# Attention scores in 64x64 quarters, and a ninth gate/up block by seven products, in a one-core decoder layer

## Chip, core and metric

The kernel runs on one NeuronCore of a Trainium2 chip. The metric is the device time of one execution in microseconds. All products run on TensorE (PE); VectorE (DVE), ScalarE (ACT), GpSimd (POOL) and the DMA queue of SyncE (SP) feed it and read its banks.

## What is computed

One layer of a hybrid decoder, 512 tokens, 1024 features, float32:

```python
h = rms_norm(x, g_mix[l]);  z = h @ w_in[l]          # q, k, v, u, gate_a, gate_s
a = dilated_attention(q, k, v, g_q[l], g_k[l])       # windows (128,1), (512,4), (2048,16), 8 heads of 64
y = gelu(s5_ssm(u, ...))
s_out = (y @ w_glu_a[l]) * sigmoid(y @ w_glu_b[l])
mix = sigmoid(gate_a) * (a @ w_attn_proj[l]) + sigmoid(gate_s) * s_out
x = x + mix @ w_out[l]
h2 = rms_norm(x, g_ffn[l])
x = x + (silu(h2 @ w_ffn_gate[l]) * (h2 @ w_ffn_up[l])) @ w_ffn_down[l]     # 2816 hidden features
```

Scores are masked: with dilation 1, query q of a block sees keys q to 127 of the block before and keys 0 to q of its own.

## The kernel before, in words

The order of the work is written out by hand, one program for each engine, with semaphores between them. Each engine works strictly in its program's order. Weights come in tiles of 256 rows by 512 columns (`w_raw`, four buffers). ACT rounds a tile to `w_hi` (`hi`, L654), DVE subtracts to `w_lo` (`lo`, L660), two buffers each, and PE multiplies in three terms: hi by hi, hi by lo, lo by hi.

**Attention.** A loop goes over four pairs of heads. In it PE has ten steps `u`. Even steps up to 6 begin with `scores(i, n)` for query block n = u/2: the two heads lie in partitions 0 to 63 and 64 to 127 of `qT` and `kT` and write banks 4 and 5 of PSUM. A block needs three products for each head: dilation 1 (for n of 1 to 3 over 256 keys, the block before and its own), dilation 4 (128 keys) and dilation 16 (128 keys, where only classes of 32 positions see each other). Each step then has one or two products of the gate projection (six matmuls of 512 columns each), and `turn_prob(i, u - 1)`: three transposes of a unit's probabilities into bank 6. A unit is one head of one block, so 8 a pair. Steps 5 and 9 end with `values` of two blocks. DVE reads the scores of each unit with two masked reductions (L1257, L1259), after which `misc_dve` reaches `md_scores(unit)`; ACT takes the exponentials (L801, L804) and copies the transposed probabilities (L818). `scores` waits for its bank head by head:

```python
                    if n:
                        pe.wait_ge(misc_dve, MD_S + md_scores(2 * n - 2 + h) + MD_PAIR * i)
```

On DVE, step 4 ends with a `lo` of a gate tile, and the reductions of unit 5 stand behind it; the `hi` that this `lo` waits for stands on ACT behind the L818 copy of unit 3.

**Gate and up.** The 2816 hidden features make 11 blocks of 256. `FP = 3` of them are plain: `ffn(f, j)` has four tiles j of 24 matmuls of 512 columns (L1832) into banks 0 to 3, and DVE takes the banks with `columns_out` (L1390). The norm of `h2` is only known late: `x1_sums` stands on PE after tile 1, the spread of the norm over the partitions (L1847) after tile 2, and DVE copies it to `norm_all` (L1409). The other 8 blocks take seven products for eight (Strassen and Winograd), `seven(f)`: 14 steps of 12 matmuls of 256 columns (L1870). For each step i, DVE and ACT round an operand of weights (`op_hi`, `op_lo` L1427), of which some are sums that POOL makes (`block_sums`) once tiles 0 and 2 of the block have landed. Once, ahead of the first such block, DVE makes the other side: the normalised activations (`normed`, L1415, eight), four differences of them (`difference`, L1486), and the low parts of seven partners (`partner_lo`, L1423) with `partner_hi` on ACT (L894). SP issues the block's tiles (`blocks`, L451) as `lo` of the plain tiles frees their buffers: tile 2 of the first such block after `lo` of the third tile of the last plain block.

Of the kernel before, what the change touches and what calls it, by code (L numbers as in the profile page):

```python
# [14 lines left out]
P = 128  # L15
# [3 lines left out]
KT = DM // P  # L19
# [26 lines left out]
W_FFN = W_OUT + 8  # L46
FP = 3
W_DOWN = W_FFN + 4 * FP
# [14 lines left out]
def build(nc, t):  # L63

    with ExitStack() as ctx:
# [599 lines left out]
        def _(act):  # L665
# [221 lines left out]
            def partner_hi(i):  # L887
                if i in (0, 5, 6):
                    act.wait_ge(hn_done, KT)
                else:  # L890
                    act.wait_ge(t_done, {1: 2, 2: 3, 3: 4, 4: 1}[i])
                if i >= 3:
                    act.wait_ge(gemm_steps, 4 * (W_DOWN - 4 + i - 3) + 4)
                nc.scalar.activation(partner(i, 0), partner_raw(i), ACT.Copy).then_inc(b_hi_done, 1)  # L894
# [40 lines left out]
            silus(0, 2)  # L935
            for j in range(1, 5):
                hi(W_FFN + j + 4, j)
                if j >= 3:
                    partner_hi(j - 3)
            for m in range(2):  # L940
                act.wait_ge(ffn_evac, 4 + m + 1)
                nc.scalar.activation(sg[:, m], sg[:, m], ACT.Silu).then_inc(silu_done, 1)
            for j in range(1, 4):
                hi(W_FFN + j + 8, j)
                if j < 3:
                    partner_hi(j + 1)
            for i in range(3):
# [8 lines left out]
            for m in range(2):  # L956
                act.wait_ge(ffn_evac, 8 + m + 1)
                nc.scalar.activation(sg[:, m], sg[:, m], ACT.Silu).then_inc(silu_done, 1)
# [22 lines left out]
        def _(dve):  # L981
# [427 lines left out]
            V.tensor_copy(norm_all[:, :], ps[:, 5]).then_inc(norm2_eps, 1)  # L1409
            lo(W_FFN + 4, 4)  # L1410
            dve.wait_ge(norm2_eps, 2)
            swiglu(0)

# [66 lines left out]
            def difference(n):  # L1480
# [5 lines left out]
                V.tensor_tensor(t_raw[n], a, b, ALU.subtract).then_inc(t_done, 1)  # L1486

            lo(W_FFN + 5, 1)
            for k in range(KT):
                normed(k)  # L1490
            lo(W_FFN + 6, 2)
            for n in range(3):
                difference(n)
            lo(W_FFN + 7, 3)
            difference(3)
            partner_lo(0)
            lo(W_FFN + 8, 4)
            partner_lo(1)
            swiglu(1)
            for j in range(1, 4):  # L1500
                lo(W_FFN + j + 8, j)
                if j < 3:
                    partner_lo(j + 1)
            for i in range(3):
# [35 lines left out]
        def _(pe):  # L1540
# [172 lines left out]
            def scores(i, n):  # L1713

                heads = (slice(0, 64), slice(64, 128))
                k0 = 0 if n else P
                q = slice(n * P, (n + 1) * P)
                for h in range(2):
                    if n:
                        pe.wait_ge(misc_dve, MD_S + md_scores(2 * n - 2 + h) + MD_PAIR * i)  # L1720
                    T.matmul(ps[:, 4 + h, k0:256], qT[heads[h], 0, q], kT[heads[h], 0, n * P - P + k0:n * P + P],  # L1721
                             start=True, stop=True)
                for g in (1, 2):
                    for h in range(2):
                        ins = T.matmul(ps[:, 4 + h, (g + 1) * P:(g + 2) * P], qT[heads[h], g, q], kT[heads[h], g, q],  # L1725
                                       start=True, stop=True)
                        if g == 2:
                            ins.then_inc(scores_done, 1)

            def turn_prob(i, u):  # L1730
                pe.wait_ge(prob_done, 8 * i + u + 1)
                if u:
                    pe.wait_ge(misc_act, MA_Y + ma_probT(u - 1) + MA_PAIR * i)
                for x in range(0 if u // 2 else 1, 3):
                    ins = T.transpose(ps[:, 6, x * P:(x + 1) * P], prob[u % 4][:, x * P:(x + 1) * P], ident[:, :])  # L1735
                ins.then_inc(prob_turned, 1)
# [78 lines left out]
            for c in range(2):  # L1815
                run(columns(W_OUT + 4 * c, 4, by_feature, h_acts, by_dve(DE_GLU + 4) if c == 0 else lambda m: None,
                            split_rows(mix_lo_done, 0), 4 * c))
            def ffn(f, j):
                w = W_FFN + j + 4 * f
                pe.wait_ge(w_lo_done, w + 1)  # L1820
                for m in range(4):
                    if j == 0:
                        if isinstance(f, int):
                            pe.wait_ge(dve_evac, DE_MIX + m + 1)
                        else:
                            pe.wait_ge(ffn_evac, 4 * f - 3 + m)
                    if isinstance(f, int) and m == 0:
                        pe.wait_ge(h2_lo_done, 2 * j + 2)
# [14 lines left out]
            ins.then_inc(x1_sums, 1)  # L1843
            ffn(0, 2)
            pe.wait_ge(norm2_done, 1)
            for n in range(TB):
                ins = T.matmul(ps[:, 5, n * P:(n + 1) * P], norm_row[:, n:n + 1].to_broadcast([P, P]), ident[:, :],  # L1847
                               start=True, stop=True)
            ins.then_inc(norm2_spread, 1)
            ffn(0, 3)  # L1850
            with pe.Fori(1, FP) as f:
                for j in range(4):
                    ffn(f, j)
# [91 lines left out]
```

## Time and profile before

| what | value |
|---|---|
| median of 3 runs | 857.26 us (856.96 to 857.64) |
| the profiled execution | 857.08 us |
| its span, first to last instruction | 855.3 us |
| PE busy | 848.7 us (99%) |
| DVE, ACT, POOL busy | 571.8, 361.2, 250.2 us |
| mean DMA rate | 127 GB/s |

The profiled execution lies 0.18 us under the median, and 1.8 us of it lie outside the span. Busy shares are means over the whole span; which engine waits for which is read from single stretches.

### The profile page before, as it was taken

To read this page: it belongs to the slowest core of one execution; us is meant where nothing else is said; L and a number is where in the kernel's file an instruction comes from. 1 tells how busy PE (TensorE), PEld (TensorE's weight loads), DVE (VectorE), ACT (ScalarE), POOL (GpSimd) and SP (SyncE) were. 2 spreads that over 40 slices of the span, in tenths; PEclk is the share of its full clock that TensorE was granted. 3 is DMA by queue.
4 is the path that set the end of the run, shared out by engine and by line. 5 is a ranking of instruction groups with operands and counts; after the bars stand their busy time and mean duration, and the time that the engine had idled before them with its cause. 6 is when DMAs were issued, how large, how long until landed. Compare 5 with 4: busy or idle time off the path is not lost.

```text
span 855.3 us, 15076 instructions
## 1 busy us (share of the span) xinstructions
PE 848.7 (99%) x5171; PEld 729.5 (85%) x5171; DVE 571.8 (67%) x790; ACT 361.2 (42%) x575; POOL 250.2 (29%) x266
## 2 busy tenths in 40 slices
PE   9999999999999999999999999999999999999998
PEld 8888788888887888888877888889999999888886
DVE  6458976567934564545587666889999999533334
ACT  6312353313345665756333343444545544222221
POOL 0689995010020000001220220056666664000000
PEclk9999999999999999999999999999999999999999
DMA  8439237634465543512635232332334333322212
GB/s 312 148 107 238 75 123 147 216 121 137 132 220 161 172 139 107 169 50 78 179 118 197 78 105 89 100 88 85 113 109 115 105 98 114 103 93 92 92 70 98
DMA packets 103494, 108.87 MB, mean 127 GB/s; under 512 B 11712, under 2 KB 69296, under 8 KB 103328
## 3 DMA queue, kind: packets, MB, share of 16 engines
q1 hardware_dynamic: 96544, 94.25, 35.4%
q10 hardware_dynamic: 5504, 10.52, 3.8%
q0 software_dynamic: 1408, 3.61, 1.9%
q8 instruction: 22, 0.36, 0.2%
q14 instruction: 16, 0.13, 0.0%
HBM read 94.38 MB, written 13.96 MB: 127 GB/s over the span
## 4 chain that ended last, share of the span: by engine, by line
PE 93%; DVE 4%; issue 1%; POOL 1%; ACT 0%; DMA 0%; SPq 0%; ACTq 0%; POOLq 0%
PE ps L1555 46%; PE ps L1870 18%; PE ps L1890 13%; PE ps L1832 6%; PE ps L1750 2%; PE ps L1779 1%; PE ps L1721 1%; PE ps L1735 1%; DVE early L1075 1%; PE ps L1725 1%; PE ps L1591 1%; PE ps L1602 1%; DVE late L1537 1%; DVE w_lo L1427 1%; DVE h_lo L1423 1%
## 5 line engine op out<-in xcount | busy, mean ns | idle before, releaser
L660 DVE TENSOR_TENSOR w_lo<-w_raw,w_hi 128x1024 fp32r<-128x1024 f32 x109 | 139.3, 1278 | 204.7 <-ACT w_hi L654 204.7
L654 ACT ACTIVATE w_hi<-w_raw 128x1024 fp32r<-128x1024 f32 x109 | 115.3, 1058 | 282.1 <-PE ps L1555 160.3
L1555 PE MATMUL ps<-w_hi,hT_hi 128*128 128x512 f32 x280 | 109.6, 392 | 0.7 <-DVE early L993 0.7
L1555 PE MATMUL ps<-w_hi,hT_lo 128*128 128x512 f32 x280 | 109.0, 389 | 0.0
L1555 PE MATMUL ps<-w_lo,hT_hi 128*128 128x512 f32 x280 | 109.0, 389 | 0.0
L1555 PE MATMUL ps<-hT_hi,w_hi 128*128 128x512 f32 x224 | 91.8, 410 | 0.0
L1555 PE MATMUL ps<-hT_hi,w_lo 128*128 128x512 f32 x224 | 87.7, 392 | 0.0
L1555 PE MATMUL ps<-hT_lo,w_hi 128*128 128x512 f32 x224 | 87.4, 390 | 0.0
L498 POOL TENSOR_TENSOR early<-early 128x16 f32<-128x16 f32 (+5 forms) x125 | 76.0, 608 | 9.7
L1870 PE MATMUL ps<-h_hi,w_hi 128*128 128x256 f32 x256 | 72.8, 285 | 0.6 <-DVE w_lo L1427 0.5
L1870 PE MATMUL ps<-h_lo,w_hi 128*128 128x256 f32 x256 | 72.4, 283 | 0.0
L1870 PE MATMUL ps<-h_hi,w_lo 128*128 128x256 f32 x256 | 72.4, 283 | 0.0
L1870 PE MATMUL ps<-hT_hi,wx_t 128*128 128x256 f32 x384 | 71.7, 283 | 0.0
L1890 PE MATMUL ps<-hT_hi,w_hi 128*128 128x512 f32 x176 | 68.5, 389 | 0.0
L1890 PE MATMUL ps<-hT_lo,w_hi 128*128 128x512 f32 x176 | 68.5, 389 | 0.0
L1890 PE MATMUL ps<-hT_hi,w_lo 128*128 128x512 f32 x176 | 68.5, 389 | 0.0
L1555 PEld LDWEIGHTS ps<-w_hi,hT_hi 128*128 128x128 f32 x280 | 52.6, 188 | 12.8 <-DVE early L993 1.5
L1555 PEld LDWEIGHTS ps<-w_lo,hT_hi 128*128 128x128 f32 x280 | 52.6, 188 | 11.1
L1555 PEld LDWEIGHTS ps<-w_hi,hT_lo 128*128 128x128 f32 x280 | 52.6, 188 | 10.8
L1870 PEld LDWEIGHTS ps<-hT_hi,wx_t 128*128 128x128 f32 x384 | 61.0, 192 | 0.0
L1870 PE MATMUL ps<-hT_lo,wx_t 128*128 128x256 f32 x192 | 54.3, 283 | 0.0
L1870 PEld LDWEIGHTS ps<-h_hi,w_hi 128*128 128x128 f32 x256 | 49.1, 192 | 1.3 <-DVE w_lo L1427 0.9
(249 smaller groups left out, 1793.0 us busy)
## 6 DMA issues: line engine op xcount, KB each, us to landing
w_raw<-in_w_in SPq DMA_DIRECT2D x108, 256.0 KB, 3.7
w_raw<-in_w_ffn_down SPq DMA_DIRECT2D x44, 256.0 KB, 2.8
w_raw<-in_w_ffn_gate SPq DMA_DIRECT2D x64, 128.0 KB, 2.2
w_raw<-in_w_ffn_up SPq DMA_DIRECT2D x64, 128.0 KB, 2.4
z_d<-early ACTq DMA_DIRECT2D x7, 1024.0 KB, 5.0
late<-z_d SPq DMA_DIRECT2D x96, 64.0 KB
w_raw<-in_w_out SPq DMA_DIRECT2D x16, 256.0 KB, 3.0
late<-z_d SPq DMA_DIRECT2D x12, 256.0 KB
```

Of the source, the lines that this page charges most:

```text
L498: tab(pool.tensor_tensor(out, a, b, op))
L654: nc.scalar.activation(w_hi[:, j % WSPL], w_raw[:, j % WRAW], ACT.Copy).then_inc(w_hi_done, 1)
L660: nc.vector.tensor_tensor(w_lo[:, j % WSPL], w_raw[:, j % WRAW], w_hi[:, j % WSPL].bitcast(F32), ALU.subtract).then_inc(w_lo_done, 1)
L1075: V.tensor_tensor(out, a, b, op).then_inc(table_prods, 1)
L1423: V.tensor_tensor(partner(i, 1), partner_raw(i), partner(i, 0).bitcast(F32), ALU.subtract).then_inc(b_lo_done, 1)
L1427: V.tensor_tensor(op_at(i, 1), op_raw(i, p), op_at(i, 0).bitcast(F32), ALU.subtract).then_inc(op_lo_done, 1)
L1537: V.tensor_tensor(y_out[:, m], x1[:, m], ps[:, m], ALU.add).then_inc(out_done, 1)
L1555: ins = T.matmul(ps[:, bank0 + m], lhsT, rhs, start=first and h == 0 and k == 0, stop=last and h == 1 and k == 2)
L1750: ins = T.matmul(ps[h * HD:(h + 1) * HD, 7, n % 2 * 256 + s * P:n % 2 * 256 + (s + 1) * P], vt[b][:, g, key, h * HD:(h + 1) * HD], turned_ ...
L1832: ins = T.matmul(ps[:, m], (w_hi, w_lo)[b][:, j % WSPL, at_w:at_w + P], (h2_hi, h2_lo)[a][:, 2 * j + h, :], start=j == 0 and h == 0 and k ...
L1870: ins = T.matmul(ps[:, BANK[i], g * 256:g * 256 + 256], op_at(i, b)[:, h * 256 + g * P:h * 256 + g * P + P], partner(i, a)[:, 2 * p + h], ...
L1890: ins = T.matmul(ps[:, m], (w_hi, w_lo)[b][:, j % WSPL, m * P:(m + 1) * P], h_acts[a][:, j % 2, :], start=first and k == 0, stop=last and ...
```

## The change

Three edits are made together.

- `scores` for blocks 1 to 3 is cut in two halves of 64 queries, c = 0 and 1. With the two heads this gives products of 64 rows by 64 columns of the array, four for each dilation. Each half takes only the keys that its queries can see: 192 of 256 for dilation 1, 128 for dilation 4, 64 of 128 for dilation 16.
- The waits of `scores` for its banks are gone. In their place `turn_prob` waits ahead of its third transpose, for units 0, 2 and 4, until DVE has read unit 1, 3 or 5.
- `FP` is 2. The spread of the second norm moves inside the third tile of the first plain block, and the preparation of the partners is reordered on ACT and DVE to fit beside one plain block.

```diff
-FP = 3
+FP = 2
...
             silus(0, 2)
-            for j in range(1, 5):
+            for j in range(1, 4):
                 hi(W_FFN + j + 4, j)
-                if j >= 3:
-                    partner_hi(j - 3)
-            for m in range(2):
-                act.wait_ge(ffn_evac, 4 + m + 1)
-                nc.scalar.activation(sg[:, m], sg[:, m], ACT.Silu).then_inc(silu_done, 1)
-            for j in range(1, 4):
-                hi(W_FFN + j + 8, j)
                 if j < 3:
-                    partner_hi(j + 1)
+                    partner_hi(j - 1)
+            for i in (2, 3):
+                partner_hi(i)
             for i in range(3):
                 op_hi(FP, 0, i, True)
...
             V.tensor_copy(norm_all[:, :], ps[:, 5]).then_inc(norm2_eps, 1)
-            lo(W_FFN + 4, 4)
             dve.wait_ge(norm2_eps, 2)
-            swiglu(0)
...
+            for k in range(4):
+                normed(k)
+            lo(W_FFN + 4, 4)
+            for k in range(4, KT):
+                normed(k)
+            columns_out(0)
             lo(W_FFN + 5, 1)
-            for k in range(KT):
-                normed(k)
-            lo(W_FFN + 6, 2)
+            gated(0)
             for n in range(3):
                 difference(n)
+            partner_lo(0)
+            lo(W_FFN + 6, 2)
+            difference(3)
+            partner_lo(1)
             lo(W_FFN + 7, 3)
-            difference(3)
-            partner_lo(0)
-            lo(W_FFN + 8, 4)
-            partner_lo(1)
-            swiglu(1)
-            for j in range(1, 4):
-                lo(W_FFN + j + 8, j)
-                if j < 3:
-                    partner_lo(j + 1)
+            for i in (2, 3):
+                partner_lo(i)
             for i in range(3):
                 op_lo(FP, 0, i)
...
-                k0 = 0 if n else P
-                q = slice(n * P, (n + 1) * P)
-                for h in range(2):
-                    if n:
-                        pe.wait_ge(misc_dve, MD_S + md_scores(2 * n - 2 + h) + MD_PAIR * i)
-                    T.matmul(ps[:, 4 + h, k0:256], qT[heads[h], 0, q], kT[heads[h], 0, n * P - P + k0:n * P + P],
-                             start=True, stop=True)
-                for g in (1, 2):
-                    for h in range(2):
-                        ins = T.matmul(ps[:, 4 + h, (g + 1) * P:(g + 2) * P], qT[heads[h], g, q], kT[heads[h], g, q],
-                                       start=True, stop=True)
-                        if g == 2:
-                            ins.then_inc(scores_done, 1)
+                for g in range(3):
+                    for c in range(2 if n else 1):
+                        first, count = ((64 * c, 192) if n else (P, P), (256, P), (384 + 64 * c, 64) if n else (384, P))[g]
+                        key = n * P + first - (P, 256, 384)[g]
+                        m = slice(64 * c, 64 * c + 64) if n else slice(0, P)
+                        for h in range(2):
+                            ins = T.matmul(ps[m, 4 + h, first:first + count], qT[heads[h], g, n * P + m.start:n * P + m.stop],
+                                           kT[heads[h], g, key:key + count], start=True, stop=True)
+                            if g == 2 and c == (1 if n else 0):
+                                ins.then_inc(scores_done, 1)
...
                 for x in range(0 if u // 2 else 1, 3):
+                    if x == 2 and u in (0, 2, 4):
+                        pe.wait_ge(misc_dve, MD_S + md_scores(u + 1) + MD_PAIR * i)
                     ins = T.transpose(ps[:, 6, x * P:(x + 1) * P], prob[u % 4][:, x * P:(x + 1) * P], ident[:, :])
...
-            ffn(0, 2)
+            ffn(0, 2, (0, 1))
             pe.wait_ge(norm2_done, 1)
             for n in range(TB):
                 ins = T.matmul(ps[:, 5, n * P:(n + 1) * P], norm_row[:, n:n + 1].to_broadcast([P, P]), ident[:, :],
                                start=True, stop=True)
             ins.then_inc(norm2_spread, 1)
+            ffn(0, 2, (2, 3))
             ffn(0, 3)
```

PE before, from `turn_prob` of unit 4 (step 5) to the scores of block 3 (step 6); `late` is the arena that holds `prob`, `qT`, `kT` and the values:

```order
L1735 MATMUL ps<-ident,late 128x128 [waits misc_act]
L1735 MATMUL ps<-ident,late 128x128 x2
L1743 ISA [waits class_turned,misc_act]
L1750 MATMUL ps<-late 64x128 [waits zt_v_in]
L1750 MATMUL ps<-late 64x128 x5
L1750 MATMUL ps<-late 64x128 [waits class_turned,misc_act]
L1750 MATMUL ps<-late 64x128 x7
L1720 REGISTER_ALU
L1721 MATMUL ps<-late 128x256 [waits misc_dve]
L1720 REGISTER_ALU
L1721 MATMUL ps<-late 128x256 [waits misc_dve]
L1725 MATMUL ps<-late 128x128 x4
```

PE of the change at the same place, where the lines are numbered by the changed file:

```order
L1730 MATMUL ps<-ident,late 128x128 [waits misc_act]
L1730 MATMUL ps<-ident,late 128x128
L1729 REGISTER_ALU
L1730 MATMUL ps<-ident,late 128x128 [waits misc_dve]
L1738 ISA [waits class_turned,misc_act]
L1745 MATMUL ps<-late 64x128 [waits zt_v_in]
L1745 MATMUL ps<-late 64x128 x5
L1745 MATMUL ps<-late 64x128 [waits class_turned,misc_act]
L1745 MATMUL ps<-late 64x128 x7
L1718 MATMUL ps<-late 64x192 x4
L1718 MATMUL ps<-late 64x128 x4
L1718 MATMUL ps<-late 64x64 x4
```

The wait for `misc_dve` has moved from the scores of block 3 to the third transpose, ahead of the 14 value products. In both programs it asks for unit 5.

DVE before, from the copy of `norm_all` on; `late` holds `x1`, `hn`, the differences and the blocks' results:

```order
L1409 COPY norm_all<-ps 128x512 [waits norm2_spread]
L660 TENSOR_TENSOR w_lo<-w_raw,w_hi 128x1024 [waits w_hi_done]
L1390 TENSOR_TENSOR late<-ps,norm_all 128x512 [waits gemm_steps,norm2_eps]
L1390 TENSOR_TENSOR late<-ps,norm_all 128x512 [waits gemm_steps] x3
L1397 TENSOR_TENSOR late<-late 128x512 [waits ffn_evac,silu_done] x2
L660 TENSOR_TENSOR w_lo<-w_raw,w_hi 128x1024 [waits w_hi_done]
L1415 SCALAR_TENSOR_TENSOR late<-late,small,norm_all 128x512 x8
L660 TENSOR_TENSOR w_lo<-w_raw,w_hi 128x1024 [waits w_hi_done]
```

DVE of the change from the same copy to the `lo` of tile 2 of the last plain block:

```order
L1404 COPY norm_all<-ps 128x512 [waits norm2_spread]
L1408 SCALAR_TENSOR_TENSOR late<-late,small,norm_all 128x512 [waits norm2_eps]
L1408 SCALAR_TENSOR_TENSOR late<-late,small,norm_all 128x512 x3
L660 TENSOR_TENSOR w_lo<-w_raw,w_hi 128x1024 [waits w_hi_done]
L1408 SCALAR_TENSOR_TENSOR late<-late,small,norm_all 128x512 x4
L1385 TENSOR_TENSOR late<-ps,norm_all 128x512 [waits gemm_steps] x4
L660 TENSOR_TENSOR w_lo<-w_raw,w_hi 128x1024 [waits w_hi_done]
L1392 TENSOR_TENSOR late<-late 128x512 [waits ffn_evac,silu_done] x2
L1479 TENSOR_TENSOR late<-late 128x1024 [waits hn_done]
L1479 TENSOR_TENSOR late<-late 128x1024 [waits t_done,hn_done] x2
L1416 TENSOR_TENSOR hT_lo<-late,hT_hi 128x1024 [waits b_hi_done]
L660 TENSOR_TENSOR w_lo<-w_raw,w_hi 128x1024 [waits w_hi_done]
```

The eight `normed` now stand ahead of `columns_out` (L1385), and all the preparation lies beside one plain block, where two had it before.

## Rows read from the trace of the kernel before

**Rows 1.** The page: the span; PE's busy tenths and granted clock in 40 slices.
```profile
span 855.3 us, 15076 instructions
PE   9999999999999999999999999999999999999998
...
PEclk9999999999999999999999999999999999999999
```

**Rows 2.** Timeline of PE, scores of block 1: start, us, rows*columns.
```profile
261.54 0.70 PE L1721 MATMUL ps<-late 64*128 64x256 f32 x4
262.07 0.61 PE L1725 MATMUL ps<-late 64*128 64x128 f32 x8
262.61 0.50 PE L1555 MATMUL ps<-hT_hi,w_hi 128*128 128x512 f32 x1
```

**Rows 3.** Timeline of PE, products of the SSM that already run as quarters.
```profile
237.66 1.16 PE L1699 MATMUL ps<-early 64*64 64x64 f32 x64
238.75 0.38 PE L1706 MATMUL ps<-early 128*128 128x128 f32 x1
```

**Rows 4.** Timeline of PE, steps 4 to 6 of the first pair.
```profile
270.17 0.49 PE L1735 MATMUL ps<-ident,late 128*128 128x128 f32 x3
...
271.88 0.49 PE L1735 MATMUL ps<-ident,late 128*128 128x128 f32 x3
272.31 1.75 PE L1750 MATMUL ps<-late 128*64 128x128 f32 x28
273.98 0.84 PE L1721 MATMUL ps<-late 64*128 64x256 f32 x4
```

**Rows 5.** Timelines of ACT and DVE at the same place.
```profile
270.69 0.49 ACT L818 ACTIVATE late<-ps 128x384 f32<-128x384 f32 x1
271.08 1.05 ACT L654 ACTIVATE w_hi<-w_raw 128x1024 fp32r<-128x1024 f32 x1
...
272.16 1.23 DVE L660 TENSOR_TENSOR w_lo<-w_raw,w_hi 128x1024 fp32r<-128x1024 f32 x1 [2.12 <-ACT w_hi L654]
...
273.64 0.42 DVE L1259 CUSTOM_DVE_ANT_0 late<-ps,masks 128x256 f32<-128x256 f32 x1
```

**Rows 6.** Timelines of DVE and PE: the end of unit 3, the transposes of unit 2.
```profile
265.52 0.09 DVE L1259 DVE_READ_ACCUMULATOR2_ANT late<- 128x1 f32 x1
...
267.16 0.49 PE L1735 MATMUL ps<-ident,late 128*128 128x128 f32 x3
```

**Rows 7.** Timeline of PE in the gate/up stage, at the starts that count.
```profile
519.49 1.05 PE L1847 MATMUL ps<-ident,norm_row 128*128 128x128 f32 x8
...
525.85 0.39 PE L1832 MATMUL ps<-h_hi,w_hi 128*128 128x512 f32 x1
...
569.37 0.28 PE L1870 MATMUL ps<-hT_hi,wx_t 128*128 128x256 f32 x1
...
578.68 0.39 PE L1870 MATMUL ps<-h_hi,w_hi 128*128 128x256 f32 x1 [0.52 <-DVE w_lo L1427]
...
611.19 0.28 PE L1870 MATMUL ps<-hT_hi,wx_t 128*128 128x256 f32 x1
...
711.99 0.28 PE L1870 MATMUL ps<-hT_hi,wx_t 128*128 128x256 f32 x1
```

**Rows 8.** Timeline of DVE in the same stage.
```profile
520.58 0.69 DVE L1409 COPY norm_all<-ps 128x512 f32<-128x512 f32 x1 [4.91 <-PE ps L1847]
...
529.00 5.38 DVE L1415 SCALAR_TENSOR_TENSOR late<-late,small,norm_all 128x512 f32<-128x512 f32 x8
...
535.44 3.88 DVE L1486 TENSOR_TENSOR late<-late 128x1024 f32<-128x1024 f32 x3
...
554.40 1.23 DVE L660 TENSOR_TENSOR w_lo<-w_raw,w_hi 128x1024 fp32r<-128x1024 f32 x1 [2.43 <-ACT w_hi L654]
...
568.18 2.47 DVE L1390 TENSOR_TENSOR late<-ps,norm_all 128x512 f32<-128x512 f32 x4
...
576.85 1.78 DVE L1427 TENSOR_TENSOR w_lo<-late,w_hi 128x512 fp32r<-128x512 f32 x1
```

More of the change, by code:

```diff
@@ L956, in _ @@
             for m in range(2):
-                act.wait_ge(ffn_evac, 8 + m + 1)
+                act.wait_ge(ffn_evac, 4 * FP - 4 + m + 1)
                 nc.scalar.activation(sg[:, m], sg[:, m], ACT.Silu).then_inc(silu_done, 1)
@@ L1817, in _, with ffn @@
                             split_rows(mix_lo_done, 0), 4 * c))
-            def ffn(f, j):
+            def ffn(f, j, columns=range(4)):
                 w = W_FFN + j + 4 * f
                 pe.wait_ge(w_lo_done, w + 1)
-                for m in range(4):
+                for m in columns:
                     if j == 0:
-                        if isinstance(f, int):
+                        if f == 0:
                             pe.wait_ge(dve_evac, DE_MIX + m + 1)
@@ L1826, in ffn @@
                             pe.wait_ge(ffn_evac, 4 * f - 3 + m)
-                    if isinstance(f, int) and m == 0:
+                    if f == 0 and m == 0:
                         pe.wait_ge(h2_lo_done, 2 * j + 2)
@@ L1849, in _ @@
             ins.then_inc(norm2_spread, 1)
+            ffn(0, 2, (2, 3))
             ffn(0, 3)
-            with pe.Fori(1, FP) as f:
+            for f in range(1, FP):
                 for j in range(4):
```

## The prediction

> **What bounds the kernel now.** I read the page first. PE is busy in every slice of the span [rows 1], so a change pays by what it takes from PE's program, and any wait that it puts into that program is lost unless PE would have waited there anyway. Then I read PE's timeline in the two stages that are edited, for the price of each product, and beside it the timelines of ACT and DVE, for when the semaphores that PE waits for are reached.
>
> **Scores by quarters: what is removed.** Scores of a block from 1 to 3 now take from 261.54 to 262.61, 1.07 us [rows 2]. Each float32 product shows as two matmuls, and those of the two heads start together: the eight matmuls of 128 columns are four pairs, (0.61 - 0.27) / 3 = 0.11 apart (a matmul of 128 columns lasts 0.27 of that), which is 0.83 ns a column and 5 ns more. So the stream is 2 x (256 + 128 + 128) columns, and what is left of 1.07 is a first weight load of about 0.11 and the drain ahead of the next matmul.
>
> Do four quarters also start together? The SSM's products answer: 64 matmuls of 64x64 in 1.16 us, of which the last lasts 0.22 [rows 3]. The starts fill 0.94 us, that is 0.058 for each four: 64 columns at 0.83 ns and 5 ns more. Four quarters cost what one does. A block's scores then are a weight load of half the columns (0.053), 2 x 0.165 for 192 columns, 2 x 0.112 for 128, one step of 0.058 to the last four, 0.02 for their skew, and 0.15 to the next matmul (237.66 + 0.94 to 238.75 [rows 3]): 0.83 us. Saved: 0.24 us, twelve times (three blocks, four pairs), **-2.9 us**. The bounds are -3.2 (the columns and the half weight load in full: 0.213 + 0.054 each) and +4.9 (halves one behind the other, below).
>
> **The moved wait.** This is the term that decides. In the pair shown, the transposes of unit 4 start at 271.88, and the third at 271.88 + 0.49 - 0.27 = 272.10 [rows 4]. It will wait for DVE to have read unit 5, whose second reduction ends at 273.64 + 0.42 = 274.06 [rows 5]. Nothing in the change brings that forward: the reductions stand behind a `lo` (272.16), that behind a `hi` on ACT (271.08), that behind the copy of unit 3 (270.69), and that behind PE's transposes of unit 3, which begin at 270.17 and end near 270.66 [rows 4, 5]. From there to the third transpose PE has one product, which the change leaves as it is. The cheaper scores pull both sides forward alike. So PE stands from 272.10 to about 274.13 (0.07 for the semaphore), and a transpose that starts anew pays its weight load, some 0.1: **2.13 us**. What is queued behind it on PE are all the value products (28 matmuls, 1.68 us) and the scores of block 3; DVE and ACT wait for these scores, but are 2 us ahead by then and cost nothing more.
>
> Before, the same semaphore was asked for after the value products, at 273.98, and cost little: the four dilation 1 matmuls there take 0.84 instead of 0.70 [rows 2, 4], 0.14 us. That goes away. The waits moved for units 0 and 2 are free: for unit 2, unit 3 is read at 265.61 and its transposes start at 267.16 [rows 6]; unit 0 has the same order of work. So a pair gains 3 x 0.24 + 0.14 = 0.86 and loses 2.13: +1.27, and in four pairs, which have one instruction stream and the same spacing, **+5.0 us**. Bounds of the wait: 0 (met in time) to 2.4 us (if the rest of a matmul's latency is exposed).
>
> **One more block by seven products.** A plain block takes (569.37 - 525.85) / 2 = 21.76 us, 0.2267 for each of 96 matmuls and 5.44 a tile; a block by seven products takes (711.99 - 611.19) / 5 = 20.16 us [rows 7]. In steady state the swap gives **-1.60 us**. The spread moves on PE from behind tile 2 into its middle and costs PE the same.
>
> What has to be ready is the question. Put on the clock of before: the spread starts 12 matmuls sooner, at 519.49 - 2.72 = 516.77, and the copy of `norm_all` 1.09 later [rows 7, 8], at 517.86. DVE then runs, with durations from [rows 5, 8]: copy and its own semaphore to 518.65; four `normed` at 0.66 to 521.3; the `lo` of tile 4, whose `hi` cannot start before tile 2 ends (525.85 - 5.44 = 520.41, and 0.2 + 1.05 for the `hi`), 521.7 to 522.85; four `normed` to 525.5; `columns_out` at 0.60 each (2.47 for four) to 527.9. The first of these frees bank 0 at 526.2, and PE wants it at 525.85 [rows 7]: **+0.4 us**. The `hi` of tile 5 stands on ACT behind two silus (an estimate of 0.6 each, from 0.49 for the 384 columns of L818), so its `lo` runs 528.5 to 529.65; `gated` 1.2, as two of `columns_out`; three differences 3.8; the first `partner_lo` 1.15; and the `lo` of tile 6, on which SP waits to fetch tile 2 of the first block by seven products, ends at 537.0. PE wants tile 6 at 526.25 + 10.88 = 537.13, just after.
>
> From that `lo` on everything is in the order of before: fetch, POOL's sums, operands, the last partner. Before, it ended at 554.40 + 1.23 = 555.63, 13.74 ahead of the first L1870 at 569.37, and the operand of step 6 was ready at 576.85 + 1.78 = 578.63, 23.0 later, when PE had just begun to wait (578.68) [rows 7, 8]. Now the plain blocks end at 526.25 + 21.76 = 548.0, so the `lo` is 11.0 ahead, not 13.74, and step 6 starts 2.74 later against its block than before: **+2.7 us**. Of this some 0.3 and 0.6 fall ahead of steps 3 and 5, whose operands come out of the same chain. Before, these 11 us had two plain blocks to hide in. Bounds: 0 (the fetch and the sums were not what bound) to 5. Sum of this part: -1.6 + 0.4 + 2.7 = **+1.5 us**.
>
> **Sum.** +5.0 + 1.5 (1.55 before rounding) = +6.6 us. On the profiled execution's own 857.08 (855.3 of span and 1.8 around it) that is 863.7; on the median of 857.26, 863.8, which I give.
>
> **A rule that speaks against quarters.** In rows, 64 small matmuls start in 0.94 us, 15 ns each [rows 3], so the 24 matmuls of a block's scores are not bound by their number. The Trainium skill, page "TensorE: Matmul & The Clock Gate", section "Wait - 56ns, not 53.3ns?", says that where the engine's sequencer decodes matmuls itself it spends about 62 ns on each, which binds once the products are shorter than that. By that page 24 of them would take 1.5 us and the sum would come out near 874 us; the trace of this case does not agree with it.
>
> **Rivals.**
> - *The wait is met in time* (chance 0.07). Should unit 5 be read before the third transpose, the wait costs nothing; the point of decision is 272.10 against 274.06. Then attention gains 4 x 0.86 = 3.5, and with +1.5 the time is 855.3 us, faster. For it: DVE idles 2.12 us ahead of the `lo` [rows 5], so it has room. Against: that idleness is a wait for ACT, which the change does not touch.
> - *The preparation fits* (0.18). If fetch and sums follow the `lo` with slack, the third block's -1.6 stays whole: 857.26 + 5.0 - 1.6 = 860.7 us. For it: DVE does 11 us of work here and idled often. Against: PE already waited at step 6 with two blocks to prepare in [rows 7].
> - *The halves don't overlap* (0.05). Then 768 columns in place of 512 stream: the 0.82 us of stream become 1.23, +0.41 a block instead of -0.24, twelve times +7.8: 871.6 us. Against it: [rows 3].
> - *The preparation is later still* (0.10): a `lo` that misses its `hi`, or slower DVE work beside POOL, some 2.7 us more: 866.5 us.
>
> **How the numbers follow.** My forecast, stall and late preparation both, has 0.60, with a range of its own of 862 to 866. The range of 859.9 to 866.7 takes in the second and fourth rival and leaves out the first and third, 0.12, and tails of the forecast. A difference under 0.2% (1.7 us, 855.5 to 859.0) could not be told from no change here. Slower by more: 0.90 (forecast, rivals two to four, less 0.03 for cases in between); same 0.04 (half of the rival with the met wait lies about there); faster 0.06.
>
> **What the profile would show.** Right: PE idle ahead of the third transpose in step 5, about 2 us in each pair, released by DVE's L1259 or its successor; scores of blocks 1 to 3 at 0.83 us; the loop over pairs longer by 1.3 us each; the first block by seven products waiting some 3.5 us in sum, most at step 6. Wrong: no idle time there, quarters that start 0.16 apart in twos, or a first block without waits. The forecast would also fail if a stall of 2 us let PE's granted clock, full in all slices of before [rows 1], fall to its lower level afterwards.

## The result, and the profile after

The changed kernel takes **867.31 us** (median of 4 runs, 867.16 to 867.51), against 857.33 (4 runs) of the kernel before on the same chip: ratio 1.0115, interval 1.0101 to 1.0129. It is 10.0 us slower, where 6.6 were forecast, and 0.6 us past the end of the range. The profiled execution took 867.16 us, 10.1 more than that of before.

The page of the kernel after, to be laid beside [rows 1]: PE's busy tenths and its granted clock in 40 slices.

```profile
span 865.4 us, 15616 instructions
...
PE   9999999999999999999999999989999999999998
...
PEclk9999999999999999999999999999999999999999
```

PE is busy nearly everywhere, as before; the 27th slice, in gate/up, has lost a tenth. What else was lost is too thin for slices of 21.6 us, and stands in the timelines.

Timelines of PE and DVE of the kernel after, the first pair of heads, as [rows 2, 4, 5]: start, us.

```profile
261.88 0.89 PE L1718 MATMUL ps<-late 64*64 64x192 f32 x24
262.69 0.50 PE L1549 MATMUL ps<-hT_hi,w_hi 128*128 128x512 f32 x1
...
264.19 0.38 PE L1730 MATMUL ps<-ident,late 128*128 128x128 f32 x2
264.62 0.50 PE L1549 MATMUL ps<-hT_hi,w_hi 128*128 128x512 f32 x1
...
271.98 0.38 PE L1730 MATMUL ps<-ident,late 128*128 128x128 f32 x2
274.23 0.33 PE L1730 MATMUL ps<-ident,late 128*128 128x128 f32 x1 [1.87 <-DVE late L1254]
274.48 1.75 PE L1745 MATMUL ps<-late 128*64 128x128 f32 x28
276.16 0.89 PE L1718 MATMUL ps<-late 64*64 64x192 f32 x24
...
263.34 1.23 DVE L660 TENSOR_TENSOR w_lo<-w_raw,w_hi 128x1024 fp32r<-128x1024 f32 x1 [3.21 <-ACT w_hi L654]
...
272.26 1.23 DVE L660 TENSOR_TENSOR w_lo<-w_raw,w_hi 128x1024 fp32r<-128x1024 f32 x1 [2.08 <-ACT w_hi L654]
...
273.74 0.42 DVE L1254 CUSTOM_DVE_ANT_0 late<-ps,masks 128x256 f32<-128x256 f32 x1
```

The reader sees three things. The scores of a block take 0.82 us (261.88 to 262.69, rounded), where [rows 2] have 1.07. The third transpose starts at 274.23. Transposes follow each other 0.11 apart, so behind those of 271.98 and 272.09 it would have started at 272.20: it is 2.03 us late. DVE's L1254 begins its last reduction for unit 5 at 273.74, behind a `lo` at 272.26 that has waited for ACT. And from the transposes at 264.19 to the product at 264.62 it is 0.43 us: the product waits for the `lo` that began at 263.34. The same place in the kernel before:

```profile
264.11 0.38 PE L1735 MATMUL ps<-ident,late 128*128 128x128 f32 x2
264.29 0.50 PE L1555 MATMUL ps<-hT_hi,w_hi 128*128 128x512 f32 x1
```

There it was 0.18, so 0.25 are new here; over the four pairs it is 0.27 each.

The waits of the kernel after, PE's for the reductions: us in all, times, longest.

```profile
PE ps L1730 <- DVE late L1254: 7.5, 4, 1.9
```

Four waits, one in each pair, of 1.9 us. They are counted from the end of the transpose before, at 272.36 in the first pair; the next could have started at 272.20, as transposes overlap, so it is late by more than its wait. From one start of `scores(0)` to the next, a pair lasts 37.41, 37.37 and 38.98 us; before it was 35.95 to 35.97. The third stands out by 1.6 us. Windows of 4 us over that pair show why.

```profile
core 0: us, PE busy (x) PEld busy (x) DVE busy (x) ACT busy (x) POOL busy (x), PEclk, DMA share, GB/s
...
345.00:349.00 4.00, 2.13 (x13) 1.59 (x11) 1.91 (x5) 2.02 (x7) 0.00 (x0) 1.00 0.62 181
349.00:353.00 4.00, 4.00 (x42) 3.43 (x46) 0.00 (x0) 2.37 (x6) 0.00 (x0) 0.57 0.07 23
```

PE stood in the first window (busy 2.13 of 4 us), and in the next its granted clock is 0.57 on the mean: it was at the lower level, 1.2 GHz, from 349.04 to 352.45. The 28 value products of that pair fill 3.2 us instead of 1.7.

Timelines of PE, POOL and DVE of the kernel after in the gate/up stage, as [rows 7, 8].

```profile
534.18 0.47 PE L1827 MATMUL ps<-h_hi,w_hi 128*128 128x512 f32 x1 [0.37 <-DVE late L1385]
...
556.07 0.28 PE L1866 MATMUL ps<-hT_hi,wx_t 128*128 128x256 f32 x1
...
564.71 0.39 PE L1866 MATMUL ps<-h_hi,w_hi 128*128 128x256 f32 x1 [0.30 <-DVE w_lo L1420]
...
568.60 0.39 PE L1866 MATMUL ps<-h_hi,w_hi 128*128 128x256 f32 x1 [2.20 <-DVE w_lo L1420]
...
549.00 3.21 POOL L628 TENSOR_TENSOR late<-w_raw 128x512 f32<-128x512 f32 x1 [25.77 <-DMA w_raw<-in_w_ffn_up]
...
543.56 1.22 DVE L660 TENSOR_TENSOR w_lo<-w_raw,w_hi 128x1024 fp32r<-128x1024 f32 x1
...
550.37 0.69 DVE L1420 TENSOR_TENSOR wx_t<-w_raw,wx_t 128x512 fp32r<-128x512 f32 x1
554.28 1.10 DVE L1420 TENSOR_TENSOR wx_t<-late,wx_t 128x512 fp32r<-128x512 f32 x1 [3.22 <-ACT wx_t L906]
...
566.80 1.74 DVE L1420 TENSOR_TENSOR w_lo<-late,w_hi 128x512 fp32r<-128x512 f32 x1
```

At 534.18 PE has waited 0.4 us for `columns_out`. The first block by seven products starts at 556.07; its step 6 would be due 8.64 later (six steps of 1.44) at 564.71, but that is when step 5 begins, and step 6 follows at 568.60. Step 5 itself takes 1.44, so 2.45 us are step 6's own wait, for the operand that DVE has ready at 566.80 + 1.74 = 568.54. The `lo` at 543.56 is that of tile 6. POOL's first sum takes 3.21 us, and DVE, which was busy without a gap until 551.06, then waits 3.22 for what hangs on it. The same sum in the kernel before, begun while DVE was idle:

```profile
559.64 1.30 POOL L628 TENSOR_TENSOR late<-w_raw 128x512 f32<-128x512 f32 x1 [44.20 <-DMA w_raw<-in_w_ffn_up]
```

### The profile page after: what moved, and what is told of

Read it like the earlier page. It is cut to its first block, busy times and chain, and to the rows that moved or that the text cites. A ratio compares the mean times of both kernels' runs of the same rounds, so it can differ in the third digit from the quotient of the medians.

```text
span 865.4 us, 15616 instructions
## 1 busy us (share of the span) xinstructions
PE 846.7 (98%) x5387; PEld 729.6 (84%) x5387; DVE 581.2 (67%) x802; ACT 366.7 (42%) x585; POOL 265.5 (31%) x274
## 4 chain that ended last, share of the span: by engine, by line
PE 48%; DVE 4%; issue 1%; POOL 1%; ACT 1%; DMA 0%; SPq 0%; DVEq 0%; ACTq 0%; POOLq 0%
PE ps L1866 20%; PE ps L1886 13%; PE ps L1549 12%; PE ps L1827 2%; DVE late L1531 1%; DVE w_lo L1420 1%; DVE h_lo L1416 1%; DVE w_lo L660 0%; DVE late L1479 0%; PE ps L1745 0%; POOL late L628 0%; ACT w_hi L654 0%; DVE late L1385 0%; DVE late L1346 0%; DVE late L1408 0%
## 5 line engine op out<-in xcount | busy, mean ns | idle before, releaser
L660 DVE TENSOR_TENSOR w_lo<-w_raw,w_hi 128x1024 fp32r<-128x1024 f32 x105 | 132.6, 1263 | 198.8 <-ACT w_hi L654 198.6
L654 ACT ACTIVATE w_hi<-w_raw 128x1024 fp32r<-128x1024 f32 x105 | 111.1, 1058 | 267.8 <-PE ps L1549 165.2
L1866 PE MATMUL ps<-h_hi,w_hi 128*128 128x256 f32 x288 | 82.1, 285 | 3.3 <-DVE w_lo L1420 3.2
L1866 PE MATMUL ps<-h_hi,w_lo 128*128 128x256 f32 x288 | 81.5, 283 | 0.0
L1866 PE MATMUL ps<-h_lo,w_hi 128*128 128x256 f32 x288 | 81.5, 283 | 0.0
L1866 PE MATMUL ps<-hT_hi,wx_t 128*128 128x256 f32 x432 | 80.7, 283 | 0.0
L498 POOL TENSOR_TENSOR early<-early 128x16 f32<-128x16 f32 (+5 forms) x125 | 74.1, 593 | 9.7
L1866 PEld LDWEIGHTS ps<-hT_hi,wx_t 128*128 128x128 f32 x432 | 68.7, 192 | 0.0
L1866 PE MATMUL ps<-hT_lo,wx_t 128*128 128x256 f32 x216 | 61.1, 283 | 0.0
L1866 PEld LDWEIGHTS ps<-h_hi,w_hi 128*128 128x128 f32 x288 | 55.2, 192 | 4.4 <-DVE w_lo L1420 4.0
```

What stands on the lines that cost most here:

```text
L498: tab(pool.tensor_tensor(out, a, b, op))
L654: nc.scalar.activation(w_hi[:, j % WSPL], w_raw[:, j % WRAW], ACT.Copy).then_inc(w_hi_done, 1)
L660: nc.vector.tensor_tensor(w_lo[:, j % WSPL], w_raw[:, j % WRAW], w_hi[:, j % WSPL].bitcast(F32), ALU.subtract).then_inc(w_lo_done, 1)
L1866: ins = T.matmul(ps[:, BANK[i], g * 256:g * 256 + 256], op_at(i, b)[:, h * 256 + g * P:h * 256 + g * P + P], partner(i, a)[:, 2 * p + h], ...
```

## Experiments

Ratios are to the kernel before, run on the same chip in turn. Spacings, starts and falls of the clock are from the profiled execution of each. Where an edit isn't taken from the change's own diff, it is shown.

**1. Attention alone:** the kernel before with the new `scores` and the moved waits, both as in the change's diff; `FP = 3` and the gate/up stage stay as before.

> The attention part of the change alone: scores by quarters and the moved waits, three plain gate/up blocks as before. Theory A (the moved wait of unit 5 costs 2.09 us a pair, the quarters save 0.53 of a possible 0.79, the wait at the scores of block 3 gives back 0.15): 4 x 1.43 = +5.7, so 863.0 us, and up to 1.7 us more for each time that PE's granted clock falls to 1.2 GHz behind a stall. Theory B (the gate/up part is what costs, attention gains by its quarters): below 857.

Measured: 864.62 us, ratio 1.0081 (1.0066 to 1.0095), +7.4 us. Timeline of PE of this kernel, step 5 of the first pair:

```profile
271.60 0.38 PE L1736 MATMUL ps<-ident,late 128*128 128x128 f32 x2
273.84 0.33 PE L1736 MATMUL ps<-ident,late 128*128 128x128 f32 x1 [1.86 <-DVE late L1259]
274.10 3.01 PE L1751 MATMUL ps<-late 128*64 128x128 f32 x28
277.04 1.25 PE L1724 MATMUL ps<-late 64*64 64x192 f32 x24
```

and the window that holds it, in which the granted clock is 0.67 on the mean:

```profile
273.00:277.00 4.00, 3.16 (x29) 2.75 (x29) 0.78 (x5) 2.44 (x6) 0.00 (x0) 0.67 0.30 91
```

The same stall (the third transpose 2.03 us late), here with the lower clock behind it in the first pair (38.97 us, the others 37.36). So the fall isn't tied to the third pair: it comes behind one of four equal stalls.

**2. The moved waits alone, scores uncut,** on the kernel before.

```diff
                 for h in range(2):
-                    if n:
-                        pe.wait_ge(misc_dve, MD_S + md_scores(2 * n - 2 + h) + MD_PAIR * i)
...
                 for x in range(0 if u // 2 else 1, 3):
+                    if x == 2 and u in (0, 2, 4):
+                        pe.wait_ge(misc_dve, MD_S + md_scores(u + 1) + MD_PAIR * i)
```

> Scores as before, in whole products; only the waits are moved into the transposes. Theory A: a stall of about 2.1 us in each pair, 4 x (2.09 - 0.15) = +7.8, so 865.1 us and up to 1.7 more for each fall of the clock. Theory B (quarters cost by their number of instructions or by the wait for the gate tile, the wait is hidden): within 0.5 us of before.

Measured: 867.09 us, ratio 1.0106 (1.0090 to 1.0122), +9.9 us. Pairs last 39.56, 37.92 and 37.87 us: +1.93 without a fall of the clock, 1.6 more with one. Against experiment 1, quarters save only 0.5 a pair, not three times 0.26 = 0.78: the 0.27 of the wait for the `lo` go off it.

**3. Attention alone, with the wait for unit 5 moved behind most of the value products:** ahead of the last one of block 1. The diff is against experiment 1.

```diff
-                    if x == 2 and u in (0, 2, 4):
+                    if x == 2 and u in (0, 2):
                         pe.wait_ge(misc_dve, MD_S + md_scores(u + 1) + MD_PAIR * i)
...
                     for h in range(2):
+                        if n == 1 and blk == 3 and h == 1:
+                            pe.wait_ge(misc_dve, MD_S + md_scores(5) + MD_PAIR * i)
```

> Scores by quarters as in the change, but the wait for unit 5 stands ahead of the last value product of block 1, where PE comes about 1.8 us later. Theory A: the stall shrinks to some 0.3 us a pair, the quarters' 0.53 remain: 4 x -0.3 = -1.2, about 856.1 us. Theory B (quarters cost by themselves): 858 or more.

Measured: 856.93 us, ratio 0.9996 (0.9987 to 1.0005), granted clock 1.00 throughout the profiled execution. Timeline of PE:

```profile
271.65 0.49 PE L1736 MATMUL ps<-ident,late 128*128 128x128 f32 x3
272.07 2.26 PE L1753 MATMUL ps<-late 128*64 128x128 f32 x28
274.26 0.89 PE L1724 MATMUL ps<-late 64*64 64x192 f32 x24
```

The stall is gone, but 28 value products take 2.2 us instead of 1.7: the last still waits for unit 5. A pair lasts 35.82 us, 0.15 less than before. That shows the stall's place to be what decides, and that DVE's chain to unit 5 is the pair's bound once PE has caught up with it: cheaper scores alone only turn into a longer wait.

**4. Gate/up alone:** the changed kernel (`FP = 2` and the new order of the preparation) with `scores` and its waits put back as before.

> The gate/up part alone: two plain blocks, nine by seven products, spread inside the third tile; attention as before. Theory A (the first block by seven products waits for its preparation): -1.6 + 0.65 + 3.2 = +2.3, so 859.6 us, granted clock full throughout. Theory B (the part is good for its 1.6 us, and what it lost in the change was an after-effect of attention): 855.7.

Measured: 860.17 us, ratio 1.0032 (1.0020 to 1.0044), +2.9 us. With the +7.4 of experiment 1 that makes 10.3, and the whole change cost 10.0: the parts add, to within what one fall of the clock more or less makes. That the clock would be full throughout was wrong: in its windows of 555 to 560, 560 to 565 and 565 to 570 us the granted clock is 1.00, 0.66 and 1.00, behind the stall at step 6 (PE idle from 558.82 to 561.02).

**5. Attention alone, with DVE's `lo` of step 4 put behind the reductions of unit 5.** The waits stay where the change has them. The diff is against experiment 1.

```diff
-                        if u in (1, 4, 8):
-                            lo(W_GATE + (u + 1) // 3 + 2 - u // 8 + 4 * i, (u + 1) // 3 + 2 - u // 8)
+                        if u in (1, 5, 8):
+                            x = {1: 2, 5: 3, 8: 4}[u]
+                            lo(W_GATE + x + 4 * i, x)
```

> Attention part alone, all waits where the change has them, but on DVE the lo of the gate tile in step 4 stands behind the reductions of unit 5 and not ahead of them. Theory A (the stall is the wait for reductions that stand behind this lo): unit 5 is read near 270.3, the third transpose at 272.1 finds its semaphore reached, no idle time there and no fall of the clock. Quarters then save 0.27 + 0.26 + 0.15 a pair, those of block 1 nothing, since PE waits for the lo of a gate tile right behind them: 4 x -0.68 = -2.7, about 854.5 us. Theory B (the stall comes from something else on the way, such as PE's own wait for the exponentials): 862 or more stays.

Measured: 854.38 us, ratio 0.9970 (0.9959 to 0.9982). Timelines of PE and DVE:

```profile
271.78 0.49 PE L1737 MATMUL ps<-ident,late 128*128 128x128 f32 x3
272.20 1.75 PE L1752 MATMUL ps<-late 128*64 128x128 f32 x28
273.88 0.89 PE L1725 MATMUL ps<-late 64*64 64x192 f32 x24
...
270.56 0.09 DVE L1259 DVE_READ_ACCUMULATOR2_ANT late<- 128x1 f32 x1
272.05 1.23 DVE L660 TENSOR_TENSOR w_lo<-w_raw,w_hi 128x1024 fp32r<-128x1024 f32 x1 [1.41 <-ACT w_hi L654]
```

Unit 5 is read at 270.65, 1.3 us ahead of the third transpose; all three run together, values take 1.7 us, and the clock stays full. A pair lasts 35.30 us. One moved line on DVE turns +7.4 us into -2.5.

**6. The same, and on ACT the `hi` of step 1 put ahead of the copy of unit 0.**

```diff
+                        if u == 1:
+                            hi(W_GATE + 2 + 4 * i, 2)
                         if u >= 1:
...
-                        if u in (1, 4, 7):
+                        if u in (4, 7):
                             hi(W_GATE + u // 3 + 2 + 4 * i, u // 3 + 2)
```

> As the run before, and on ACT the hi of the gate tile in step 1 stands ahead of the copy of unit 0's transposed probabilities, so that its lo is ready some 0.9 us sooner. Theory A (the first quarters' saving of 0.26 a pair is eaten by PE's wait for that lo): another 4 x -0.26 = -1.0, about 853.5 us. Theory B (the 0.28 us on PE behind the transposes of unit 1 are a cost of quarters or of switching the array): same as the run before.

Measured: **853.05 us**, ratio 0.9957 (0.9943 to 0.9971), the fastest kernel here. Timelines of ACT and PE at the place where the changed kernel lost 0.28 us:

```profile
261.30 1.05 ACT L654 ACTIVATE w_hi<-w_raw 128x1024 fp32r<-128x1024 f32 x1
262.25 0.36 ACT L820 ACTIVATE late<-ps 128x256 f32<-128x256 f32 x1
...
264.10 0.38 PE L1739 MATMUL ps<-ident,late 128*128 128x128 f32 x2
264.23 0.48 PE L1558 MATMUL ps<-hT_hi,w_hi 128*128 128x512 f32 x1
```

The product starts 0.13 us after the first of its transposes, not 0.43. That shows the second missed term: the `hi` used to stand behind a copy that waits for PE's transposes, ahead of the scores, so that cheaper scores brought PE sooner to a `lo` that came no sooner.

**7. Gate/up alone, with the `lo` of tile 6 two operations sooner.**

```diff
-            for n in range(3):
+            for n in range(2):
                 difference(n)
-            partner_lo(0)
             lo(W_FFN + 6, 2)
+            difference(2)
+            partner_lo(0)
             difference(3)
```

> Gate/up part alone; the lo of tile 6, which lets SP fetch tile 2 of the first block by seven products, stands ahead of the third difference and the first partner and so ends some 2.4 us sooner. Theory A1 (as predicted: the chain from this lo over fetch and sums sets step 6): the wait at step 6 shrinks by as much, about 857.7 us. Theory A2 (POOL's first sum gets nowhere while DVE is busy without a gap, whenever its tiles land): the first sum ends where it did, and the time stays within 0.5 us of the gate/up part alone, 860.2.

Measured: 860.15 us, ratio 1.0037 (1.0023 to 1.0052), as experiment 4. Timelines of POOL and DVE:

```profile
540.30 4.59 POOL L628 TENSOR_TENSOR late<-w_raw 128x512 f32<-128x512 f32 x1 [24.20 <-DMA w_raw<-in_w_ffn_up]
...
543.07 0.69 DVE L1420 TENSOR_TENSOR wx_t<-w_raw,wx_t 128x512 fp32r<-128x512 f32 x1
```

The fetch lands sooner and the sum starts sooner (in experiment 4: 541.38, for 3.24 us), but it ends at 544.9 against 544.6: 1.14 us after DVE's run without a gap ended (543.75), as there (543.47). (The two executions are 0.5 us apart at the first block by seven products, so against it the sum starts some 1.6 us sooner.) This breaks the chain of my forecast, in which everything follows from the `lo` of tile 6.

**8. Gate/up alone, with POOL's first four sums made over 16 columns.** The kernel leaves out the rest of these sums (their buffers are zeroed beforehand), so it doesn't compute the whole block; it only shows what they cost.

```diff
-                pool.tensor_tensor(s1_f[p], a21, a22, ALU.add).then_inc(sum_done, 1)
+                few = (lambda a: a[:, 0:16]) if first and p == 0 else (lambda a: a)
+                pool.tensor_tensor(few(s1_f[p]), few(a21), few(a22), ALU.add).then_inc(sum_done, 1)
...
```

> Gate/up part alone; POOL makes the first four block sums over 16 columns in place of 512, the rest stays zero, so the output of that block is left out in part. Theory A (fetch and sums set the late operands of the first block): op 1 and 2 come some 3 us sooner, steps 3, 5 and 6 hardly wait, about -1.6 + 0.65 + 0.3 against before: 856.6 us. Theory B (DVE's own work for one plain block is what is too much): still 859 or more.

Measured: 856.34 us, ratio 0.9994 (0.9984 to 1.0003). Timelines of POOL and DVE:

```profile
540.66 2.26 POOL L629 TENSOR_TENSOR late<-w_raw 128x16 f32<-128x16 f32 x1 [23.80 <-DMA w_raw<-in_w_ffn_up]
543.00 0.22 POOL L631 TENSOR_TENSOR late<-late,w_raw 128x16 f32<-128x16 f32 x1
...
542.16 0.69 DVE L1424 TENSOR_TENSOR wx_t<-w_raw,wx_t 128x512 fp32r<-128x512 f32 x1
```

Even a sum of 16 columns, whose like takes 0.22 us, lasts 2.26 us and ends 0.07 after DVE's run (542.85). With the sums out of the way the stalls ahead of steps 3 and 5 are gone, and step 6 waits 0.58 us instead of 2.45: the sums are what binds the late preparation.

**9. The whole change, with both mends of attention** (the diffs of experiments 5 and 6).

> The whole change with attention mended as in the two attention runs (lo of step 4 behind unit 5, hi of step 1 ahead of the copy). If the parts add up: 853.05 us and the gate/up part's 2.9 make 856.0. If the gate/up part's late operands interact with the earlier start: off that by more than 0.8.

Measured: 856.14 us, ratio 0.9991 (0.9981 to 1.0000): experiments 6 and 4 summed (-3.8 and +2.9). The clock falls once, from 557.49 to 560.90, that is 0.25 us before the stall at step 6 ends (557.74). Of its eleven runs five have a mean granted clock of 1.000, so no fall, and four have 0.998, one fall; the five take 856.1 us on the mean, the four 857.1.

**10. Gate/up alone, POOL's sums of the second half held back to the seventh operand.**

```diff
-            pool.wait_ge(op_lo_done, 5)
+            pool.wait_ge(op_lo_done, 7)
             block_sums(FP, 1, True)
```

> Gate/up part alone, but POOL begins the second half's block sums only when all seven low parts of the first half are made, not after five. Theory (DVE and POOL take each other's time, so the sums of the second half stretch DVE's last operands of the first: 1.78, 2.30 and 1.75 us where 0.68, 1.21 and 0.68 are possible): the operand of step 6 comes 2.9 us sooner, but the sums of the second half come as much later and bring a wait of 1 to 2 us at its step 1 or 2: 858.2 us against 860.2. Rival (no contention, the chain is only in order): no change at step 6, 860.2 or more.

Measured: 859.98 us, ratio 1.0037 (1.0023 to 1.0051): expected 858.2, so a miss. Timeline of DVE, first of experiment 4, where POOL sums beside it:

```profile
555.29 1.78 DVE L1420 TENSOR_TENSOR w_lo<-w_raw,w_hi 128x512 fp32r<-128x512 f32 x1
557.00 2.30 DVE L1416 TENSOR_TENSOR h_lo<-late,h_hi 128x1024 fp32r<-128x1024 f32 x1
559.22 1.74 DVE L1420 TENSOR_TENSOR w_lo<-late,w_hi 128x512 fp32r<-128x512 f32 x1
```

and of this kernel, with PE's later wait:

```profile
555.04 0.69 DVE L1420 TENSOR_TENSOR w_lo<-w_raw,w_hi 128x512 fp32r<-128x512 f32 x1
555.65 1.22 DVE L1416 TENSOR_TENSOR h_lo<-late,h_hi 128x1024 fp32r<-128x1024 f32 x1
556.78 0.69 DVE L1420 TENSOR_TENSOR w_lo<-late,w_hi 128x512 fp32r<-128x512 f32 x1
...
562.42 0.38 PE L1865 MATMUL ps<-hT_hi,wx_t 128*128 128x256 f32 x1 [1.53 <-DVE wx_t L1420]
```

The three operations take 2.6 us instead of 5.8, and PE reaches step 6 without a wait at either 5 or 6. But the second half's operands are later by as much: its second step starts at 562.42, 1.7 late, and the next four are 1.7 apart instead of 1.44. The contention is real, and its cost only changes its place. The equal time hides one thing: this profiled execution has no fall of the clock. Its first two blocks by seven products take 45.46 us, those of experiment 4 with a fall 45.85, and those of the changed kernel, which has the same gate/up stage and no fall there, 45.04. Where the clock stays full, the later sums lose 0.4 us.

**11. The whole change with all mends:** attention as in 9, POOL as in 10, and `columns_out` ahead of the last four `normed`.

```diff
+            columns_out(0)
             for k in range(4, KT):
                 normed(k)
-            columns_out(0)
```

> The whole change with attention mended, POOL's second half later, and columns_out of the first block ahead of the last four normed (gives back the 0.4 us wait at the second block's first tile). If all add up: 853.05 + 2.9 - 2.0 - 0.3 = 853.6 us, about level with three plain blocks and mended attention.

Measured: 857.13 us, ratio 0.9997 (0.9988 to 1.0006): expected 853.6, a miss. PE no longer waits at the start of the second plain block, but its tile 6 starts 1.1 us late (at 534.49). On DVE `columns_out` now comes first and waits for PE's products (idle 0.50 and 0.67 us), and the four `normed` that used to fill that time stand behind it, all ahead of that tile's `lo`. The kernel is 1.0 us slower than that of experiment 9. The gate/up part cost time in each form that computes the whole block.

## Why the prediction was wrong

The direction was right, and so was the mechanism in attention. The missing 3.5 us are four terms: two that the sum put at nothing (the wait for a gate tile's `lo`, 1.1, and the clock, 1.6), and two in gate/up that it had too small (0.3 and 0.5). Measured terms are differences of PE's starts in the two profiled executions.

| term | forecast | measured |
|---|---|---|
| twelve blocks of scores | -2.9 | -3.1 (0.26 each) |
| wait for unit 5, four pairs | +8.5 | +8.4 (2.09 each: 2.03 of wait, 0.06 until the values start) |
| wait given back at `scores(3)` | -0.6 | -0.6 |
| wait for the gate tile's `lo` ahead of step 3 | none | +1.1 (0.27 each) |
| granted clock | none | +1.6 |
| one more block by seven products | -1.6 | -1.6 |
| first plain blocks | +0.4 | +0.7 |
| late preparation | +2.7 | +3.2 |
| ahead of the attention loop | none | +0.3 |
| sum | +6.6 | +10.0 |

The 0.3 ahead of the loop say nothing of the change: in kernels with the same code up to there the loop starts anywhere from 257.3 to 258.6.

**Scores by quarters.** Right, and the range's other end (halves one behind the other) is out: 0.82 us a block for a forecast of 0.83. The starts of the 24 matmuls fill 0.89 - 0.22 = 0.67 us, 29 ns each. The Trainium skill ("TensorE: Matmul & The Clock Gate", "Wait — 56ns, not 53.3ns?") has some 62 ns for each, 1.5 us for 24, but only for the case in which the sequencer decodes them itself. The trace does not agree with that figure, so that case does not seem to be at work here; the prediction's 874 us rested on it. What failed is the step "the cheaper scores pull both sides forward alike". It holds for what comes out of the scores; it does not for the gate tile's `lo`, whose chain starts at the transposes ahead of them. Before, that `lo` (it starts at 263.00 and takes 1.23 us) came just in time for the product at 264.29, and I had looked only at the wait that the diff names. Experiment 6, which brings that `lo` sooner, takes the wait away.

**The moved wait.** Right in place, releaser and size: the 2.03 us of waiting are those forecast, and what a restart costs was put at 0.1 and is 0.06. Experiment 5 is its proof: take away what makes unit 5 late, leave the wait where it is, and the stall is gone.

**The clock.** The forecast named this as what would make it wrong, and gave it no chance and no price. Each profiled execution with a fall (the change, experiments 1, 2, 4, 7 and 9) has it beside a stall that makes PE 2 us or more late: it begins between 0.25 us before the stall's end and 1.6 after, and lasts 3.41 us. In attention it costs 1.6 to 1.7 us, nearly the half of 3.41 that the lower level takes. In gate/up it costs 0.6 to 0.8: there PE waits for operands in the next steps even at the full clock, and the slower products fill these waits (the first two blocks by seven products take 45.60 to 45.85 us in experiments 4, 7 and 9 with a fall, 45.04 in the change without one). Before, and in experiments 3, 5, 6, 8, 10 and 11, the clock is full. Not every such stall brings a fall: the change has five and one fall, and of experiments 1, 2, 7 and 9 some runs have a mean granted clock of 1.000. The mean granted clock of the change's four runs, 0.996 to 0.998, allows for one or two falls each. What picks the stall was not tried.

**One more block by seven products.** The swap gave the forecast 1.60. In the plain blocks, "the spread costs PE the same" missed 0.12 for a second exposed weight load, since tile 2 is now cut in two, and tile 5 began another 0.13 late. In the late preparation the placing in time held: the `lo` of tile 6 ended 11.3 us ahead of the block, forecast 11.0. But the operand of step 6 came 23.8 after it, forecast 23.0. The step that failed is "from that `lo` on everything is in the order of before": it took over before's durations with before's order, and POOL's first sum took 3.21 us, not 1.30. Before, DVE was idle when that sum began; now it had a full queue. Experiments 7 and 8 show that the end of DVE's run sets the end of that sum, not the fetch. So that the forecast's 2.7 came near the measured 3.2 is in part luck: experiment 7 brought the `lo` and the fetch sooner, and the time stayed. The rival "preparation fits" falls. The rival "later still, slower DVE work beside POOL" had the right two engines, but the new delay is POOL's behind DVE (DVE's 1.78 us beside POOL stand in [rows 8] already), and its 2.7 more were too dear.

## What to carry to other kernels

A wait may be moved ahead only after asking what stands in front of its releaser: here one `lo` too early in DVE's program cost four stalls of 2.1 us, and moving it behind the reductions made the same edit pay (853.05 us with one `hi` moved too, and the plain blocks kept at three). When a step gets cheaper, check each engine's chain that starts ahead of it, since those don't get sooner with it. When preparation is squeezed into half the time, durations read where the engines idled don't hold.

## What the runs showed of the hardware

- A PE stall that makes the next product 2.0 to 2.5 us late (1.86 to 2.20 us idle between dense products) can be followed by 3.41 us in which the granted clock is 1.2 GHz. In attention that cost 1.6 to 1.7 us, most of the stall again; in gate/up 0.6 to 0.8, where PE had waits to fill. The same stall brings a fall in some runs of a kernel and none in others (experiment 9). A stall of 1.7 us (1.53 idle, experiments 10 and 11) was not followed by one.
- POOL's sum got nowhere while DVE ran operations with two SBUF inputs back to back: 128x512 took 1.30 us alone, 3.21 and 4.59 beside such a run, and 16 columns 2.26. The other way round, DVE's operations beside POOL's sums took 1.78 and 2.30 us instead of 0.69 and 1.22. The Trainium skill ("SBUF — State Buffer", "Who interferes with whom") says that a DVE instruction with two SBUF inputs contends with a GpSimd one that reads SBUF, and that the shared pair of ports is an exclusive lock. The trace agrees that they contend; it adds that POOL stayed shut out over several of DVE's instructions in a row, which the page leaves open.
